# Last two steps of a streamed expert layer: the order of the last matrices, and halves brought as quarters

## The reference

```
def expert_block(args):
    tok, e = args
    xb = x_pad[tok]
    hb = jax.nn.silu(xb @ w1[e]) * (xb @ w3[e])
    return hb @ w2[e]
...
h = layer_norm(DEEPNORM_ALPHA * h + ffn, ln2_g[l], ln2_b[l])
```

## Time and profile before

| | us |
|---|---|
| median of 3 executions (1280.99 to 1285.2) | 1283.78 |
| profiled execution, its own time | 1281.37 |
| its span | 1279.7 |
| TensorE busy in it | 1233.4 |
| VectorE busy in it | 444.8 |
| ScalarE busy in it | 319.3 |

### The profile page before, as it was taken

One profiled execution on the slowest core, in us unless ns is written; L12 is line 12 of the kernel. 1 busy time (PEld: TensorE's weight loads), 2 busy tenths in 40 slices (PEclk: granted clock), 3 DMA queues, 4 the chain that ended last, 5 costly groups with the idle time before them and its releaser, 6 DMA issues.

```text
span 1279.7 us, 15343 instructions
## 1 busy us (share of the span) xinstructions
PE 1233.4 (96%) x6669; PEld 710.7 (56%) x6669; DVE 444.8 (35%) x636; ACT 319.3 (25%) x544; POOL 7.1 (1%) x17
## 2 busy tenths in 40 slices
PE   6999999999999999999999999989998999989997
PEld 6989889988744444444444444445443444434433
DVE  7889996855410203133130211102020211111026
ACT  5443333533421211111211111111211111111212
POOL 1000000000000000000000000000000000000000
PEclk9999999999999999999999999999999999999998
DMA  8655555696999999999999999999999999999996
GB/s 310 217 186 188 171 191 184 234 383 222 351 389 422 418 423 427 425 427 428 428 428 428 426 429 428 427 427 428 428 427 428 428 428 429 427 427 428 423 411 236
DMA packets 71143, 472.28 MB, mean 369 GB/s; under 512 B 7978, under 2 KB 8562, under 8 KB 41762
## 3 DMA queue, kind: packets, MB, share of 16 engines
q1 hardware_dynamic: 70642, 470.48, 90.6%
q10 hardware_dynamic: 432, 0.79, 0.2%
HBM read 469.14 MB, written 2.10 MB: 368 GB/s over the span
## 4 chain that ended last, share of the span: by engine, by line
PE 78%; DMA 19%; DVE 2%; issue 0%; ACT 0%; SPq 0%; DVEq 0%; ACTq 0%
PE psum L912 30%; DMA ring<-in_w_dram 14%; PE psum L668 9%; PE psum L695 9%; PE psum L957 8%; PE psum L834 7%; DMA slot<-in_w_dram 5%; PE psum L624 5%; PE psum L627 2%; PE psum L870 2%; PE psum L871 2%; PE psum L992 1%; PE psum L899 1%; PE psum L811 1%; DMA area_a<-in_x_dram 1%; DVE area_b L1978 0%
## 5 line engine op out<-in xcount | busy, mean ns | idle before, releaser
L912 PE MATMUL psum<-ring,area_c 128*64 128x512 f32 x1424 | 386.8, 601 | 13.6 <-DMA ring<-in_w_dram 7.9
L912 PEld LDWEIGHTS psum<-ring,area_c 128*64 128x64 f32 x1424 | 120.9, 138 | 207.9 <-issue 204.7
L1279 ACT ACTIVATE area_c<-psum,gain 128x128 f32<-128x128 f32 x256 | 96.2, 456 | 294.7 <-PE psum L834 294.7
L1848 DVE TENSOR_TENSOR area_a<-area_a,psum 128x512 f32<-128x512 f32 x56 | 38.3, 683 | 354.6 <-PE psum L871 354.6
L1446 DVE TENSOR_TENSOR w_low<-ring,w_high 128x2048 fp32r<-128x2048 f32 x55 | 125.9, 2289 | 63.1 <-ACT w_high L1123 63.0
L1123 ACT ACTIVATE w_high<-ring 128x2048 fp32r<-128x2048 f32 x55 | 105.4, 1916 | 145.5 <-PE psum L627 42.5
L912 PE MATMUL psum<-slot,area_c 128*64 128x512 f32 x384 | 135.9, 599 | 0.0
L957 PE MATMUL psum<-ring,area_d 128*64 128x512 f32 x560 | 126.7, 594 | 4.5 <-DMA ring<-in_w_dram 4.5
L834 PE MATMUL psum<-one_hot,area_b 128*128 128x128 f32 x1024 | 124.9, 278 | 0.8 <-DVE one_hot L1775 0.8
L834 PEld LDWEIGHTS psum<-one_hot,area_b 128*128 128x128 f32 x1024 | 118.0, 192 | 13.1 <-issue 12.2
L1832 DVE TENSOR_TENSOR y_low<-psum,y_high 128x512 fp32r<-128x512 f32 x64 | 42.7, 686 | 235.8 <-ACT y_high L1288 235.8
(11 more groups left out here) (233 smaller groups left out, 1055.9 us busy)
## 6 DMA issues: line engine op xcount, KB each, us to landing
ring<-in_w_dram SPq DMA_DIRECT2D x101, 2048.0 KB, 29.7
slot<-in_w_dram SPq DMA_DIRECT2D x34, 2048.0 KB, 29.5
ring<-in_w_dram SPq DMA_DIRECT2D x46, 1024.0 KB, 10.2
ring<-in_w_in_dram SPq DMA_DIRECT2D x40, 1024.0 KB, 5.0
area_g<-in_w_dram SPq DMA_DIRECT2D x16, 2048.0 KB, 31.1
ring<-in_w_out_dram SPq DMA_DIRECT2D x16, 1024.0 KB, 5.2
slot<-in_w_dram SPq DMA_DIRECT2D x14, 1024.0 KB, 8.7
area_g<-in_w_dram SPq DMA_DIRECT2D x10, 1024.0 KB, 9.6
```

The lines of the kernel that those rows point to most:

```text
L912: mm = pe.matmul(psum[i * CAP:(i + 1) * CAP, j // UNITS, :], gathered[:, kk, i * CAP:(i + 1) * CAP], w[i][:, k, :], start=kk == 0, stop=kk ...
L1279: ins = act.activation(gathered[:, k, :], psum[:, 2 + g % 2, k % 4 * P:(k % 4 + 1) * P], ACT.Identity, scale=gain[:, 0, k:k + 1], bias=gai ...
L1848: v.tensor_tensor(area_a[:, 0, cols], area_a[:, 0, cols], psum[:, at, :], ALU.add)
```

## The change

In the last two steps the order becomes: w1 and w3 of a, w1 and w3 of b, w2 of a, w2 of b. All 20 halves from m = 168 on (all of both steps but b's w2) are brought by `load_pair` as quarters and waited for as quarters. A pair of these is loaded when the pair eight halves before it is used up. All four combines of a stand in the wide part of b's w2, one after each f, into banks 0 to 3 (`beside`). ScalarE copies b's turned matrices ahead of a's high parts, and VectorE makes b's hidden matrix ahead of a's low parts and sums. The turning of b's hidden matrix stands between f = 1 and f = 2 of a's w2. The rows of the last layer norm go to the slot of half 167, without a wait of their own.

```
-        second_rows = [sem(f"late_second_quarters_loaded{i}") for i in range(3)]
+        second_rows = [sem(f"late_second_quarters_loaded{i}") for i in range(STEP_UNITS - 2)]
...
-        LATE = STEP_UNITS * PAIRS - SLOTS - 2
-        PRODUCTS_DONE = (STEP_UNITS - 1) * (PAIRS - 2) + 4 * UNITS + FT - 1
+        LATE = STEP_UNITS * (PAIRS - 2)
+        COLUMNS = STEP_UNITS * PAIRS - UNITS
+        PRODUCTS_DONE = (STEP_UNITS - 1) * (PAIRS - 2) + 4 * UNITS
...
-        ln2_slot = slots[slot_of(LATE + 4)]
+        ln2_slot = slots[slot_of(STEP_UNITS * PAIRS - 2 * SLOTS - PLACES)]
...
-            for m in range(SPLIT_FILLS, LAST):
+            for m in range(SPLIT_FILLS, LATE):
                 unit_used((m - PLACES) // STEP_UNITS, (m - PLACES) % STEP_UNITS)
                 load_expert_unit(m, m % STEP_UNITS, m // STEP_UNITS)
-            for n in range(SLOTS - 2):
-                unit_used(PAIRS - 2, n)
-                if n < HALF // 2:
-                    load_expert_unit(LAST + n, n, PAIRS - 1)
-                else:
-                    load_expert_unit(LAST + n, n + UNITS, PAIRS - 2)
...
-            unit_used(PAIRS - 2, SLOTS - 2)
-            load_pair(LATE, STEP_UNITS - 2, PAIRS - 2)
+            for m in range(LATE, LATE + 2 * SLOTS, 2):
+                unit_used((m - SLOTS) // STEP_UNITS, (m - SLOTS) % STEP_UNITS)
+                load_pair(m, (m - LATE) % SLOTS, PAIRS - 2 + (m - LATE) // SLOTS)
             for j in range(0, UNITS, 2):
                 last_unit_used(j)
-                load_pair(LAST + SLOTS + j, UNITS + j, PAIRS - 1)
+                load_pair(LAST + SLOTS + j, 2 * UNITS + j, PAIRS - 2)
...
-            sp.wait_ge(y_ready, NC * (PAIRS - 1))
+            last_unit_used(SLOTS - 2)
...
             with sp.Else():
-                sp.wait_ge(experts_done, PRODUCTS_DONE)
                 load_ln2_rows()
...
-                elif LATE <= m < LATE + 6:
+                elif LATE <= m < COLUMNS:
                     pe.wait_ge(second_rows[(m - LATE) // 2], 16 * 2)
...
-            def combine(it, c):
+            def combine(it, c, beside=False):
...
-                    bank = COMBINED[c % 2] + t
+                    bank = (2 * (c % 2) if beside else COMBINED[c % 2]) + t
...
-                unit_products(b, b % TWO, lambda j: arrived(start + 2 * UNITS + j), False, units=range(UNITS))
-                for f in range(FT):
-                    hidden_rows(f, arrived(start + 3 * UNITS + f))
-                pe.wait_ge(silu_ready, PAIRS)
-                for t in range(TT):
-                    pe.transpose(psum[:, 0, t * P:(t + 1) * P], one_hot[:, b % TWO, t, :], ident[:])
-                pe.wait_ge(s_last_rows, 16 * 2)
-                pe.transpose(psum[:, 0, TT * P:TT * P + 2 * CT], last_rows_2,
-                             ident[0:2 * CT, 0:2 * CT]).then_inc(gt_ready, 1)
-                for j in range(UNITS, 2 * UNITS):
-                    unit_products(b, b % TWO, lambda j: arrived(start + 3 * UNITS + j), False, units=(j,))
-                    if j in (UNITS, 2 * UNITS - 1):
-                        first = 0 if j == UNITS else NC // 2
-                        combine(a, first)
-                        combine(a, first + 1)
+                for j in range(2 * UNITS):
+                    unit_products(b, b % TWO, lambda j: arrived(start + 2 * UNITS + j), False, units=(j,))
+                    if j == UNITS:
+                        pe.wait_ge(silu_ready, PAIRS)
+                        for t in range(TT):
+                            pe.transpose(psum[:, 0, t * P:(t + 1) * P], one_hot[:, b % TWO, t, :], ident[:])
+                        pe.wait_ge(s_last_rows, 16 * 2)
+                        pe.transpose(psum[:, 0, TT * P:TT * P + 2 * CT], last_rows_2,
+                                     ident[0:2 * CT, 0:2 * CT]).then_inc(gt_ready, 1)
+                for f in range(FT // 2):
+                    hidden_rows(f, arrived(start + 4 * UNITS + f))
...
+                for f in range(FT // 2, FT):
+                    hidden_rows(f, arrived(start + 4 * UNITS + f))
                 pe.wait_ge(half_kept, 1)
+                pe.wait_ge(ht_drained, PAIRS)
...
-                pe.wait_ge(comb_added, NC * b - 1)
+                pe.wait_ge(y_drained, NC * a + 2)
                 for f in range(FT):
-                    if f == FT // 2:
-                        pe.wait_ge(ht_drained, PAIRS)
                     for c in range(2):
                         last_rows(f, c, [wide[i][:, f, c, :] for i in range(2)], s_wide)
+                    combine(a, f, True)
                 pe.wait_ge(y_drained, NC * b)
...
-                for c in range(NC):
-                    keep_y_high(it - 1, c)
-                    if c == 1:
-                        act.wait_ge(gt_ready, PAIRS)
-                        act.activation(last_gain, psum[:, 0, TT * P:TT * P + 2 * CT], ACT.Copy)
-                        act.activation(one_hot_t_2[:], halves(psum[:, 0, 0:TT * P]), ACT.Copy).then_inc(gt_drained, 1)
+                act.wait_ge(gt_ready, PAIRS)
+                act.activation(last_gain, psum[:, 0, TT * P:TT * P + 2 * CT], ACT.Copy)
+                act.activation(one_hot_t_2[:], halves(psum[:, 0, 0:TT * P]), ACT.Copy).then_inc(gt_drained, 1)
...
+                for c in range(NC):
+                    keep_y_high(it - 1, c)
...
-                if it == PAIRS - 1:
-                    for c in range(0, NC, 2):
-                        for i in range(2):
-                            keep_y_low(it - 1, c + i)
-                        if c == 0:
-                            for i in range(2):
-                                add_combined(it - 1, i, COMBINED[i])
                 hide(it, it == PAIRS - 1)
-            for i in range(2):
-                add_combined(PAIRS - 2, 2 + i, COMBINED[i])
+            for c in range(0, NC, 2):
+                for i in range(2):
+                    keep_y_low(PAIRS - 2, c + i)
+                for i in range(2):
+                    add_combined(PAIRS - 2, c + i, 2 * i)
```

## The result

| kernel | median us (executions) | ratio to before, 95% interval | profiled: own time, span |
|---|---|---|---|
| before | 1283.28 (8) | | 1281.37, 1279.7 |
| changed | 1286.81 (8) | 1.0025 (1.0017 to 1.0034) | 1285.38, 1283.6 |

The change costs 0.25% of 1283.28, or 3.2 us (2.2 to 4.4). Forecast were 3.7 us, 0.29%, with a chance of 0.53 for a change within 0.3% and 0.42 for slower. The spans of the two profiled executions differ by 3.9 us. Their starts agree up to step a: TensorE's f = 2 of step 13 begins at 1140.93 in one and at 1140.88 in the other, so the two traces can be laid on each other from there.

A forecast was written before the change was run, and what follows sets the result against it. The DMA stream of experts' weights was taken as the limit up to the last awaited arrival, TensorE after it. Slower quarters +1.3 and work behind that arrival +2.4 make +3.7 us: 1283.78 becomes 1287.5, range 1282.5 to 1291.5.

The forecast's parts named there:

- TensorE's lead at step a goes into waits: At the start of step a quarters remove 4.4 us of delay, worth nothing at the end: waits before later arrivals.
- Quarters slow the stream, +1.3 us: In the weight stream 14 more halves come as quarters, at 419 instead of 427 GB/s: last arrival +1.3 us.
- t: Landing of the 20th 2 MB arrival from half 168 on, at 1239.26 us before; TensorE is the limit from there.
- Behind t, +2.4 us: From the 20th arrival's landing to b's first combine: 17.5 to 17.8 us against 15.21, +2.3 to +2.6, taken as +2.4.
- The two combines more and the dropped turning: TensorE's work behind the 20th arrival: two more combines of a, 0.69 us less of turning and copy; +1.76 us.
- The waits for VectorE: Behind the 20th arrival TensorE waits 0.25 us before a's third combine, then for VectorE again before b's first combine.
- SyncE, nothing: SyncE issues 14 more DMAs, 5 to 6 us in all over some 90 us mostly spent waiting: cost nothing.
- The sum: Whole kernel: +1.3 for the stream and +2.4 behind the last arrival give +3.7 us, a median of 1287.5 us.
- The clock did not fall behind 1215 us: Rival: TensorE's clock falls just before the end, slower, +5.4 us with one fall, +7.1 with two; chance 0.14.
- the lead was not kept: Rival: time won at the start of step a reaches the end, -2.8 us without slower quarters, 1281.0; chance 0.10.
- quarters were not free: Rival: quarters cost the weight stream nothing, so only +2.4 us remains, 1286.2 us; chance 0.13.
- the combines did not fill waits for columns: Rival: b's columns come late, a's four combines stand in those waits, only the stream counts: +1.3, 1285.1; chance 0.05.

The follow-up runs named there:

- the middle of the stream: Kernel before with each of halves 31 to 181 brought by two quarter DMAs split by columns, still waited for whole: ratio 1.0087 to before.
- thin combines: Changed kernel with a's four combines in the last part thinned to 64 of 512 columns each: ratio 1.0005 (0.9996 to 1.0015) to before.
- one low part ahead: Changed kernel with VectorE reading the overflow flag first and making b's first low part before a's fourth sum: ratio 1.0027 to before.
- The two parts measured alone: Against the kernel before: new order with halves 168 to 181 whole, 1.0013 (1.7 us); old order with all halves from 168 as quarters, 1.0010 (1.3 us).

## Why the prediction was right

- **TensorE's lead at step a goes into waits.** Right. Step a starts at 1147.77 (forecast 1148.0), and six waits of 1.03 to 1.42 us follow, where five or six of 0.9 to 1.5 were forecast. The first pair alone as quarters leaves the time at 0.9995 (0.9986 to 1.0004).
- **Quarters slow the stream, +1.3 us.** Right in the mechanism, and closer in the number than its working deserved. t moved by 1.23 us in this execution, but quarters by themselves cost about 1.0: 14 times the 0.074 us a half of the middle of the stream, 1.0 in the old order with quarters, and 1.0 in the profiled execution of thin combines, whose stream of 99.4 us has the new order too. The other 0.3 us here are two arrivals of 2 MB that came 5.06 and 5.18 us behind the one ahead (1200.44 and 1235.46), with 4.94 to 4.99 for the rest. Other executions have such an arrival in another place (5.94 us at 1158.09 in the one with one low part ahead), so I take this for chance of the execution. The 419 GB/s of 390 to 450 us, on which the forecast rested, held such a thing too: a quarter that landed 3.3 us behind the one ahead, with 2.5 for the others. In the long stretches quarters run at 421. The Trainium skill's 341 GB/s for a transfer of 1 MB ("DMA: Bandwidth & Descriptors", section "Measured (HBM→SBUF, 128 partitions, SWDGE, issued from GpSimd)") isn't what queued 1 MB transfers reach here.
- **Behind t, +2.4 us.** Right in the mechanism; measured 2.65, just above the 2.3 to 2.6 given. The two combines more and the dropped turning were sized at +1.76; there is also some 0.5 us in the groups of eight, which take 1.85 to 1.87 us each with a combine between them and not the 1.76 of an unbroken run; the forecast has nothing for it, and no run shows its cause. The waits for VectorE were forecast at 0.25 and 0.2 to 0.5, and are 0.18 and 0.27, by the distance of starts (2.05 and 2.14 where 1.87 is the distance without a wait). Thin combines confirm that TensorE's part is in the stretch (-2.3 us), one low part ahead the last wait (-0.2 us).
- **SyncE, nothing.** Right in the cost, wrong in the working: 14 issues more were put at 5 to 6 us in all, and the 40 issues of quarters took 83 us. The lead of 24.2 us and more covered it.
- **The sum.** 1.23 + 2.65 = 3.9 us is the whole difference of the two spans. The timed ratio says 3.2 (2.2 to 4.4), which both this and the 3.7 fit. The two parts measured alone, 1.7 and 1.3 us, add up to 3.0. That the sum came so near is in part luck: the quarters were forecast 0.3 us too high, the stretch 0.25 us too low, and these two errors cancel.
- **The rivals.** The clock did not fall behind 1215 us in the profiled execution; the lead was not kept; quarters were not free; the combines did not fill waits for columns (the last wide piece landed at 1250.65, TensorE began its last quarter of the wide part at 1253.21).

## What to carry to other kernels

Where a stream of weights is the limit, find the last arrival that something waits for: work done sooner ahead of it buys nothing, and the work behind it adds to the end (2.65 us of stretch were 1.7 us, 0.5 to 2.8, in the time). Let waits ahead of it take what is not urgent (one combine moved there: stretch 15.21 to 14.29 us), and don't group by matrix so that what is left to do for the step before (here its combines) lands behind it. A finer wait ahead of that arrival bought nothing and cost 0.07 us a half here; what it is worth at that arrival itself, which came as quarters in every version, no run tests.

## What the runs showed of the hardware

A stream of DMAs over 64 partitions each, first and second half in turn, ran at 219 to 221 GB/s from 500 to 1200 us, half of the 428 of DMAs over 128, with a DMA share of 1.01 in both. It is no fixed price: later in the same execution the same kind of transfers ran at 359 (1600 to 1700 us), and the cause of either stays open. The Trainium skill ("DMA: Bandwidth & Descriptors", section "Rules for kernel authors") says of two transfers to disjoint partition halves that both "spray across all 16 SDMA engines" and that one 128-partition transfer is to be used; the share agrees with the first, and the trace adds that all the engines' time was used for half the rate over those 700 us.

Two quarters of 1 MB landed every 4.97 us (421 GB/s), a half of 2 MB every 4.89 us (428). With 40 quarters issued one behind the other an issue took 2.13 us of SyncE in the median; it was 0.43 for the quarters of the earlier trace rows and 0.35 for the halves that L418 brings into `ring` in the kernel before. No run shows what sets it.
